# A four-portion decoder trunk: the odd portions' convolution counted out per pair of experts, and one norm divided later

## The chip, the cores and the metric

One core of a Trainium2 chip runs the whole program. The metric is the device time of one execution in microseconds (us), the median of three runs.

## The reference, cut to what matters

Two layers run over 256 prompt rows and 32 sample rows of 1024 channels. Each layer is a mixing sublayer (three parallel branches and their gates) and an expert sublayer, which looks up 16 of 16384 one-neuron experts for each of 8 heads.

```python
glu = val_b * jax.nn.sigmoid(gate_b)
ext = jnp.concatenate([conv_past, glu], axis=1)
c = _causal_depthwise(ext, w['b_conv_w'], w['b_conv_b'])      # 31 taps
y_b = jax.nn.silu(_layernorm(c, w['b_ln_g'], w['b_ln_b']))
merged = (jax.nn.sigmoid(gl_a) * (y_a @ w['w_o_a'])
          + jax.nn.sigmoid(gl_b) * (y_b @ w['w_o_b'])
          + jax.nn.sigmoid(gl_m) * (y_m @ w['w_o_m']))
x = x + merged @ w['w_out']
...
hid = jax.nn.gelu(jnp.einsum('bd,bhkd->bhk', xb, u_tab[eid]), approximate=False)
return jnp.einsum('bhk,bhkd->bd', g * hid, v_tab[eid])        # g: softmax of the 16 best scores
```

The change touches when the 31-tap depthwise convolution is done and when its LayerNorm is divided. What is computed stays the same.

## The kernel before

The rows are cut into four portions `m` = 0 to 3: portion 0 is layer 0 of the first 128 prompt rows, portion 1 is layer 0 of the other 128 and of the 32 sample rows, and 2 and 3 are the same for layer 1. Each portion has a mixing part (function `mixing(m)`, one for each engine) and an expert part. The expert part is a row of pairs: even portions have 8 steps of 8 pairs (64 pairs), odd portions 10 steps (80 pairs). For a pair GpSimd (POOL) issues two gathers of 1 MB each (line L611) into one of five slots, VectorE (DVE) forms two dot products (`dots`, L1672), ScalarE (ACT) applies gelu and builds two diagonals (`diags`, L1036), and TensorE (PE) multiplies them with the gathered rows (`values`, L2453), which frees the slot.

While the pairs of portion `m` run, the mixing part of portion `m + 1` is done beside them. There is no scheduler on the chip: a table `PLACE[m]` gives every piece of the mixing part a place on a scale worked out from estimated costs (`glu0` .. `glu7`, attention `S`, `T`, `O`, gates `mg0` .. `mg23`, the spatial pieces `ua` and `sg`, `csum` and `csq` for the convolution's norm, `out`, `wq`, `sc`), and `reach(m, u)` says how far along it an engine may go by pair `u`. A generator per engine yields places, and the engine runs it up to `reach` after each pair. PE goes one pair further than DVE and ACT: it does mixing work after the value products of pair `u`, which DVE and ACT meet after the dot products of pair `u + 1`. Every engine runs its own list in order, so an instruction that waits holds all behind it on its engine.

On DVE the order within a pair is: dot products; then one of the selection's parts by the pair's number `k` in its step (`k` = 0 `pick_pairs`, 1 `pick_experts`, 3 `gates`, 5 `scale_fold`, 6 and 7 `pick_half`; at `k` = 2 and 4 there is none, and the mixing part goes there); for `k` = 2 of every other step `add_group` (L1695); then the mixing part up to `reach`. The convolution of 31 taps over 8 blocks of 128 channels is cut into 62 steps of four instructions each (`convolve`, L1141 for the first tap, L1143 for the others). In the kernel before, the mixing code itself calls `conv(taps)` with small numbers, in front of its attention, gate and spatial pieces, and a last `conv(2 * CONV_W)` in front of `centre` takes what is left. The sample rows' convolution runs beside `glu`: POOL multiplies (L638, four products per block of channels) and DVE sums (`sample_taps`, L1151).

The norm behind the convolution is `centre` (`csum`, L1448), ACT's squares, and `norm_c` (`csq`): DVE scales PE's sum of squares (L1454), ACT takes the root, DVE takes its reciprocal (L1456) and multiplies (L1458), and ACT's `swish` follows. Pairs are counted below from the start of the expert part beside which the mixing runs, from 0 to 63 beside portions 0 and 2.

Of the kernel before, what the change touches and what calls it, by code (L numbers as in the profile page):

```python
# [19 lines left out]
CONV_W = 31  # L20
# [10 lines left out]
PORTIONS = 2 * DEPTH  # L31
# [5 lines left out]
STEPS = (8, 10)  # L37
FIRST = [sum(STEPS[i % 2] for i in range(m)) for m in range(PORTIONS + 1)]
NSTEP = FIRST[PORTIONS]
PAIRS = 8  # L40
# [26 lines left out]
CACHED = (0, 3)  # L67
# [27 lines left out]
for _k, _c in WKIND:  # L95
# [14 lines left out]
    conv=(1, 1), pe_csum=(1, 1), cd=(1, 1), csq=(1, 1), pe_csq=(1, 1), cvar=(1, 1), rt_c=(1, 1), cn=(1, 1), yb=(8, 8),  # L110
# [16 lines left out]
def at(name, m, k):  # L127
    return sum(per(name, i) for i in range(m)) + k
# [61 lines left out]
PLACE = []  # L190
# [27 lines left out]
def reach(m, u):  # L218

    last = PAIRS * STEPS[(m - 1) % 2] - TAIL  # L220
    place = PLACE[m]
    if u >= last:

        return place.get(f"sc{u - last + 1}", 1e9)
    if m == 1:

        return place["glu0"] + (place["sc1"] - place["glu0"]) * (u + 1) / (last + 1)
    return place["sc1"] * (u - LEAD) / (last - LEAD)

# [11 lines left out]
def build(nc, x_in, consts_in, mem_in, cache_in, state_in, w_in, small_in, vecs_in, fing_in, ws_in, wss_in,  # L241
          keys_in, uv_in, y_out, memk_out, memv_out, convp_out, convs_out, vn_out):
    with ExitStack() as ctx:
# [857 lines left out]
        def _(dve):  # L1101
# [29 lines left out]
            def mixing(m):  # L1131
# [21 lines left out]
                done = [0]  # L1153

                def conv(n):

                    for _ in range(n):
                        if done[0] < 2 * CONV_W:
                            convolve(4 * (done[0] // CONV_W), (done[0] % CONV_W,))
                            done[0] += 1  # L1160

# [24 lines left out]
                for c in range(KB):  # L1186
# [17 lines left out]
                    if m == 0 and c == 2:  # L1204
                        dve.wait_ge(S["memsq"], 1)
                        V.tensor_reduce(rb_mem, kT.rearrange("p c t -> p t c"), AX.X, ALU.add).then_inc(S["memred"], 1)
                    if p == 0 and c == (4 if m == 0 else 2):
                        dve.wait_ge(S["pe_memsq"], at("pe_memsq", m, 1))
                        V.tensor_scalar(rb_mem, s_bank[0][:, 0:M], 1.0 / D, EPS, ALU.mult, ALU.add).then_inc(S["memvar"], 1)
# [35 lines left out]
                def beside(name, taps):  # L1245
                    yield place[name]
                    conv(taps)
# [44 lines left out]
                else:  # L1292
# [35 lines left out]
                    if m == 1:  # L1328
                        conv(2)
# [22 lines left out]
                def gated(first, last, taps):  # L1352
                    for c in range(first, last):

                        yield place[f"mg{c + 1}"] + 2 if c % 8 == 0 else place[f"mg{c}"]
                        conv(taps)
# [63 lines left out]
                def spatial():  # L1420
                    for i in range(3):
                        yield from beside(f"ua{i}", 1 if m == 3 else 2)
                    for i in range(4):
# [3 lines left out]
                        conv((2, 1, 2, 0)[m])  # L1427
# [23 lines left out]
                def norm_c():  # L1451
                    yield place["csq"]
                    dve.wait_ge(S["pe_csq"], at("pe_csq", m, 1))
                    V.tensor_scalar(rb[:, 0:nt], t_bank[:, 0:nt], 1.0 / D, EPS, ALU.mult, ALU.add).then_inc(S["cvar"], 1)  # L1454
                    dve.wait_ge(S["rt_c"], at("rt_c", m, 1))
                    V.reciprocal(rb[:, 0:nt], rb[:, 0:nt])  # L1456
                    dve.drain()
                    V.tensor_tensor(yB[:, :, 0:nt], yB[:, :, 0:nt], rb[:, 0:nt].unsqueeze(1).to_broadcast([P, KB, nt]), ALU.mult).then_inc(S["cn"], 1)  # L1458
# [19 lines left out]
                else:  # L1478
                    taps = 1 if m in CACHED else 2
                    yield from gated(0, 3, taps)  # L1480
                    yield from norm_v_gain()
                    yield from gated(3, 5, taps)
                    yield from norm_v_bias()
                    yield from gated(5, 8, taps)
                    yield from spatial()
                    yield from gated(8, 12, 3 if m in CACHED else 4)
                    conv(2 * CONV_W)
                    yield from centre()
                    yield from gated(12, 14, 0)
                    yield from norm_c()  # L1490
                    yield from gated(14, 24, 0)
# [245 lines left out]

            V.memset(one, 1.0).then_inc(one_set, 1)
# [9 lines left out]
            for m in range(PORTIONS):  # L1748
                mix = first if m == 0 else stepper(mixing(m + 1)) if m + 1 < PORTIONS else None
                for u in range(PAIRS * STEPS[m % 2]):  # L1750
# [22 lines left out]
                    if k == 2 and s % 2 == 0 and s:  # L1773
                        add_group(s // 2 - 1)
                    if mix:
                        mix(reach(m + 1, u - 1))
# [796 lines left out]
```

## Time and profile before

| | us |
|---|---|
| median of 3 runs (lowest, highest) | 2237.01 (2234.17, 2238.07) |
| the profiled execution | 2238.65 |
| its span, first to last instruction | 2236.9 |
| PE busy | 1631.0 (73%) |
| DVE busy | 1567.8 (70%) |
| POOL busy | 721.5 (32%) |
| ACT busy | 656.0 (29%) |

The DMA engines moved 895.56 MB at 400 GB/s on average. The page cuts the span into 40 equal slices of 56 us. A group or row of the trace names the line, the engine, the operation, what it writes and reads, and in brackets how long the engine stood idle before it and what it then got. Matmul ends are modelled, so a busy PE is not a PE at its peak.

### The profile page before, as it was taken

To read this page: it belongs to the slowest core of one execution; us is meant where nothing else is said; L and a number is where in the kernel's file an instruction comes from. 1 tells how busy PE (TensorE), PEld (TensorE's weight loads), DVE (VectorE), ACT (ScalarE), POOL (GpSimd) and SP (SyncE) were. 2 spreads that over 40 slices of the span, in tenths; PEclk is the share of its full clock that TensorE was granted. 3 is DMA by queue.
4 is the path that set the end of the run, shared out by engine and by line. 5 is a ranking of instruction groups with operands and counts; after the bars stand their busy time and mean duration, and the time that the engine had idled before them with its cause. 6 is when DMAs were issued, how large, how long until landed. Compare 5 with 4: busy or idle time off the path is not lost.

```text
span 2236.9 us, 31355 instructions
## 1 busy us (share of the span) xinstructions
PE 1631.0 (73%) x10944; PEld 1069.0 (48%) x10944; DVE 1567.8 (70%) x4170; ACT 656.0 (29%) x1647; POOL 721.5 (32%) x660
## 2 busy tenths in 40 slices
PE   9999987788797477878788647766999853334334
PEld 9866675566675055554433415543887610000002
DVE  4464269988766667877775577787876686776775
ACT  3121232421414242432132323342223332322222
POOL 0000056332232433342222234531323254454443
PEclk9999998899898588999899757876999865555556
DMA  9699899999899999999999999999999999999997
GB/s 338 250 385 402 335 406 420 384 418 400 327 410 419 422 420 421 422 412 422 421 390 421 421 421 414 409 393 396 420 417 421 409 400 421 422 421 421 422 421 317
DMA packets 127773, 895.56 MB, mean 400 GB/s; under 512 B 16096, under 2 KB 16928, under 8 KB 20480
## 3 DMA queue, kind: packets, MB, share of 16 engines
q0 software_dynamic: 83232, 604.02, 65.6%
q1 hardware_dynamic: 44384, 289.54, 32.1%
q8 instruction: 88, 1.44, 0.3%
q14 instruction: 69, 0.57, 0.1%
HBM read 885.39 MB, written 8.11 MB: 399 GB/s over the span
## 4 chain that ended last, share of the span: by engine, by line
PE 33%; DMA 28%; DVE 24%; issue 4%; ACT 4%; DVEq 3%; POOL 3%; SPq 0%; POOLq 0%; ACTq 0%
DMA uv<-uv_in,idx_u 22%; PE bank L1797 14%; DVE uv L1672 11%; PE bank L2109 5%; PE bank L2453 4%; DMA ring<-w_in 4%; DVE yB L1143 3%; PE bank L1803 3%; POOL uv L611 2%; DMA ring<-cache_in 2%; POOL merged L638 1%; ACT L675 1%; DVEq L1138 1%; ACT diag L1036 1%; DVE x L1695 1%
## 5 line engine op out<-in xcount | busy, mean ns | idle before, releaser
L611 POOL DMA_INDIRECT uv<-uv_in,idx_u x574 | 652.1, 1136 | 1294.5 <-PE bank L2453 634.1
L1672 DVE CUSTOM_DVE_ANT_0 uv<-uv,xrep 128x1024 f32<-128x1024 f32 x576 | 687.4, 1231 | 217.0 <-DMA uv<-uv_in,idx_u 209.6
L2453 PE MATMUL bank<-uv,diag 128*32 128x512 f32 x2176 | 393.0, 803 | 476.2 <-ACT diag L1036 470.3
L1797 PEld LDWEIGHTS bank<-xnT,ring 128*128 128x128 f32 x3168 | 434.5, 202 | 77.4 <-issue 68.3
L1797 PE MATMUL bank<-xnT,ring 128*128 128x160 f32 (+1 forms) x3168 | 456.2, 304 | 1.1 <-DMA ring<-w_in 1.0
L675 ACT ACTIVATE pick<-pick 128x2 f32<-128x2 f32 (+1 forms) x315 | 66.9, 213 | 1053.3 <-DVE pick L1672 1052.5
L2453 PEld LDWEIGHTS bank<-uv,diag 128*32 128x32 f32 x2176 | 49.4, 122 | 663.3 <-ACT diag L1036 598.0
L1143 DVE SCALAR_TENSOR_TENSOR yB<-ext_p,small,yB 128x128 f32<-128x128 f32 x960 | 275.2, 348 | 19.5
L675 ACT ACT_TABLE_LOAD x137 | 175.8, 1283 | 2.4
L1036 ACT ACTIVATE diag<-gated_fold,pick 128x32 f32<-128x32 f32 x574 | 153.1, 314 | 9.8 <-ACT pick L675 0.5
L2109 PE MATMUL bank<-ring,xnT 128*128 128x512 f32 x192 | 88.3, 615 | 0.0
L1797 PE MATMUL bank<-yMA,ring 128*128 128x160 f32 x512 | 76.8, 306 | 5.5 <-ACT yMA L675 5.5
L1797 PEld LDWEIGHTS bank<-yMA,ring 128*128 128x128 f32 x512 | 73.6, 196 | 5.7 <-ACT yMA L675 5.7
L675 ACT ACTIVATE phase<-bank 128x512 f32<-128x512 f32 (+2 forms) x44 | 23.3, 529 | 176.4 <-PE bank L1797 73.4
L1020 ACT ACTIVATE xrep<-xnf 32x1024 f32<-32x1024 f32 x64 | 67.4, 1053 | 1.4
L1803 PE MATMUL bank<-ring,ext_s 128*128 128x256 f32 x256 | 60.9, 399 | 0.0
L2446 PE MATMUL bank<-uv,diag 128*32 128x256 f32 x256 | 28.2, 586 | 43.0 <-ACT diag L1036 43.0
L2109 PEld LDWEIGHTS bank<-ring,xnT 128*128 128x128 f32 x192 | 36.8, 196 | 47.1 <-issue 46.2
L2109 PE MATMUL bank<-ring,yMA 128*128 128x512 f32 x128 | 57.0, 597 | 0.5 <-DMA ring<-w_in 0.3
L675 ACT ACTIVATE sg<-bank 128x160 f32<-128x160 f32 (+1 forms) x80 | 23.4, 293 | 115.1 <-PE bank L1797 114.9
L1797 PE MATMUL bank<-ext_s,ring 128*128 128x256 f32 x256 | 57.1, 381 | 0.0
L1803 PEld LDWEIGHTS bank<-ring,ext_s 128*128 128x128 f32 x256 | 51.1, 202 | 12.1 <-issue 4.6
(323 smaller groups left out, 1848.0 us busy)
## 6 DMA issues: line engine op xcount, KB each, us to landing
ring<-w_in SPq DMA_DIRECT2D x211, 1024.0 KB
uv<-cache_in SPq DMA_DIRECT2D x16, 1024.0 KB, 9.6
ring<-cache_in SPq DMA_DIRECT2D x16, 1024.0 KB
uv<-uv_in,idx_u POOLq DMA_INDIRECT x578, 13.9
uv<-w_in SPq DMA_DIRECT2D x4, 1024.0 KB, 10.3
ring<-w_in SPq DMA_DIRECT2D x6, 512.0 KB, 4.7
ext_s<-state_in SPq DMA_DIRECT2D x2, 1088.0 KB, 14.0
convs_out<-ext_s SPq DMA_DIRECT2D x2, 1088.0 KB, 24.7
```

What stands on the lines that cost most here:

```text
L611: nc.gpsimd.indirect_dma_start(out=uvbuf[2 * b + i], out_offset=None, in_=uv_in, in_offset=bass.IndirectOffsetOnAxis(ap=ids[:, c:c + 1], a ...
L638: ins = nc.gpsimd.tensor_tensor(taps_s[:, :, t], ext_s[:, c, :, t:t + CONV_W], wconv[:, c].unsqueeze(1).to_broadcast([P, NSEQ, CONV_W]), A ...
L675: ins = nc.scalar.activation(out, in_, func, bias=bias, scale=scale, **({} if accum is None else {"accum_out": accum}))
L1020: ins = nc.scalar.activation(xrep[gg % 2][32 * i:32 * (i + 1), :], xnf[1 if t == 2 else 0][r0:r0 + 32], ACT.Copy)
L1036: ins = nc.scalar.activation(diag[:, t % 4, i], gated_fold[:, c], ACT.Copy, scale=gel[:, 16 * (s % 2) + c:16 * (s % 2) + c + 1])
L1143: ins = V.scalar_tensor_tensor(out=yB[:, c, 0:P], in0=ext_p[:, c, w:w + P], scalar=wconv[:, c, w:w + 1], in1=yB[:, c, 0:P], op0=ALU.mult, ...
L1672: ins = V.tensor_tensor_reduce(out=u, in0=u, in1=xrep[gg % 2][:, :], scale=1.0, scalar=0.0, op0=ALU.mult, op1=ALU.add, accum_out=hid[:, c: ...
L1797: ins = MM(out, w[:, k, P * b:P * (b + 1)], rhs(k), start=k == 0, stop=k == KB - 1)
L1803: ins = MM(out, lhs(k), w[k], start=k == 0, stop=k == KB - 1)
L2109: ins = MM(out[:, :], rows[:, 4 * (i % 2) + k, 0:P], w[:, k, :], start=i % 2 == 0 and k == 0, stop=i % 2 == 1 and k == 3)
L2446: ins = MM(vbank[gg % 2][32 * q:32 * (q + 1), 0:256], diag[:, t % 4, i], uvbuf[2 * b + i][:, c:c + 256], start=first and i == 0, stop=last ...
L2453: ins = MM(vbank[gg % 2][c:c + 32, :], diag[:, t % 4, i], uvbuf[2 * b + i][:, D + 512 * n:D + 512 * (n + 1)], start=first, stop=last)
```

## The change

In odd portions (1 and 3) the convolution no longer hangs on the mixing code. `TAPS[m][u]` says how many of the 62 steps are to be done by the end of pair `u`; it shares them by the weights `HEAVY` over the pairs from the one that reaches `glu4` to two before the one that reaches `csum`. DVE calls `conv_upto` once a pair, behind the selection's part and `add_group` and ahead of the last mixing call. A step waits until `glued` says that its four blocks of `glu` are there. All other `conv` calls of odd portions fall away, but for the last one, which finds nothing left. Even portions keep theirs. The second part: in odd portions `norm_c` yields at place `mg14` between its scaling and the wait for ACT's root.

```diff
+HEAVY = (1, 1, 3, 3, 4, 3, 1, 1)
+
+def taps_by(m):
+    us = range(PAIRS * STEPS[(m - 1) % 2])
+    first = next(u for u in us if reach(m, u - 1) >= PLACE[m]["glu4"])
+    last = next(u for u in us if reach(m, u - 1) >= PLACE[m]["csum"]) - 2
+    total, so_far, out = sum(HEAVY[u % PAIRS] for u in range(first, last + 1)), 0, []
+    for u in us:
+        so_far += HEAVY[u % PAIRS] if first <= u <= last else 0
+        out.append(-(-2 * CONV_W * so_far // total))
+    return out
+
+TAPS = {m: taps_by(m) for m in range(1, PORTIONS, 2)}
...
-                done = [0]
+                done, glued = [0], [0]
...
+                def conv_upto(n):
+                    while done[0] < n and glued[0] >= 4 * (done[0] // CONV_W + 1):
+                        conv(1)
+                if p:
+                    beside_pair[0] = conv_upto
...
+                    glued[0] = c + 1
...
                 def beside(name, taps):
                     yield place[name]
-                    conv(taps)
+                    if p == 0:
+                        conv(taps)
...
-                def gated(first, last, taps):
+                def gated(first, last):
                     for c in range(first, last):
                         yield place[f"mg{c + 1}"] + 2 if c % 8 == 0 else place[f"mg{c}"]
-                        conv(taps)
                         dve.wait_ge(S["pe_proj"], at("pe_proj", m, c + 1))
...
-                        conv((2, 1, 2, 0)[m])
+                        conv((2, 0, 2, 0)[m])
...
                     V.tensor_scalar(rb[:, 0:nt], t_bank[:, 0:nt], 1.0 / D, EPS, ALU.mult, ALU.add).then_inc(S["cvar"], 1)
+                    if p:
+                        yield place["mg14"]
                     dve.wait_ge(S["rt_c"], at("rt_c", m, 1))
                     V.reciprocal(rb[:, 0:nt], rb[:, 0:nt])
...
+                    if m % 2 == 0:
+                        beside_pair[0](TAPS[m + 1][u])
                     if mix:
                         mix(reach(m + 1, u - 1))
```

The steps done in each pair, read from the two orders of DVE (four instructions each):

| portion, pairs | before | after |
|---|---|---|
| 1, 0 to 7 | 0 0 0 0 0 0 0 0 | 0 0 0 0 5 3 1 1 |
| 1, 8 to 15 | 0 4 2 2 2 1 2 3 | 1 1 3 3 4 3 1 1 |
| 1, 16 to 23 | 0 2 0 4 2 2 2 2 | 1 1 3 3 4 3 1 1 |
| 1, 24 to 31 | 2 2 2 4 1 2 2 9 | 1 1 3 3 4 3 1 1 |
| 1, 32 and 33 | 4 4 | 1 0 |
| 3, 8 to 15 | 0 0 0 0 3 1 2 2 | 0 2 3 3 4 3 1 1 |
| 3, 16 to 23 | 3 3 1 3 5 2 3 6 | 1 1 3 3 4 3 1 1 |
| 3, 24 to 31 | 4 0 3 1 1 1 1 2 | 1 1 3 3 4 3 1 1 |
| 3, 32 to 37 | 1 1 1 0 6 6 | 1 1 3 3 3 0 |

The lists of PE, ACT, POOL and SP keep their order. First place: DVE in portion 1, pair 5, the sum of a sample block. `yB` is the convolution's result, `merged` holds POOL's products, `gated_fold` the experts' weights. Before:

```order
L1672 ISA uv,pick<-uv,xrep 128x1024
L1672 ISA pick 128x1
L1684 TENSOR_TENSOR gated_fold<-consts,pick 128x256
L1151 TENSOR_REDUCE yB<-merged 128x32
L1199 TENSOR_TENSOR ext_p<-bank,sg 128x128
```

And now (line numbers of the changed kernel), from the end of pair 4:

```order
L1161 SCALAR_TENSOR_TENSOR yB<-ext_p,small,yB 128x128 x16
L1698 ISA uv,pick<-uv,xrep 128x1024
L1698 ISA pick 128x1
L1710 TENSOR_TENSOR gated_fold<-consts,pick 128x256
L1161 SCALAR_TENSOR_TENSOR yB<-ext_p,small,yB 128x128 x12
L1169 TENSOR_REDUCE yB<-merged 128x32
```

Four plus three steps moved ahead of this sum, and with the first tap's four instructions pair 4 holds five steps.

Second place: DVE in portion 1, pair 31, the last spatial product (`yMA`) and the gates 8 and 9 (`sg`, `merged`). Before:

```order
L1143 SCALAR_TENSOR_TENSOR yB<-ext_p,small,yB 128x128 x4
L1439 TENSOR_TENSOR yMA<-yMA,bank 128x320
L1143 SCALAR_TENSOR_TENSOR yB<-ext_p,small,yB 128x128 x16
L1364 SCALAR_TENSOR_TENSOR sg<-sg,bank 128x160
L1366 TENSOR_TENSOR merged<-merged,sg 128x160
L1143 SCALAR_TENSOR_TENSOR yB<-ext_p,small,yB 128x128 x16
L1364 SCALAR_TENSOR_TENSOR sg<-sg,bank 128x160
```

And now:

```order
L1161 SCALAR_TENSOR_TENSOR yB<-ext_p,small,yB 128x128 x4
L1464 TENSOR_TENSOR yMA<-yMA,bank 128x320
L1389 SCALAR_TENSOR_TENSOR sg<-sg,bank 128x160
L1391 TENSOR_TENSOR merged<-merged,sg 128x160
L1389 SCALAR_TENSOR_TENSOR sg<-sg,bank 128x160
```

The two runs of four steps each that stood between the product and the gates are gone.

Third place: DVE in portion 1, pairs 36 and 37, the norm (`rb` is the root's row). Before:

```order
L1454 TENSOR_SCALAR rb<-bank 128x160
L1456 RECIPROCAL rb<-rb 128x160
L1458 TENSOR_TENSOR yB<-yB,rb 128x1280
L1672 ISA uv,pick<-uv,xrep 128x1024
L1672 ISA pick 128x1
```

And now:

```order
L1479 TENSOR_SCALAR rb<-bank 128x160
L1698 ISA uv,pick<-uv,xrep 128x1024
L1698 ISA pick 128x1
L1710 TENSOR_TENSOR gated_fold<-consts,pick 128x256
L1483 RECIPROCAL rb<-rb 128x160
L1485 TENSOR_TENSOR yB<-yB,rb 128x1280
```

The dot products of pair 37 and its fold moved ahead of the wait for the root. In portion 3 both places are reached by the same pair, so nothing stands between the two parts there.

## Rows read from the trace of the kernel before

**Rows 1.** The page, part 2: DMA share and rate in 40 slices.

```profile
DMA  9699899999899999999999999999999999999997
GB/s 338 250 385 402 335 406 420 384 418 400 327 410 419 422 420 421 422 412 422 421 390 421 421 421 414 409 393 396 420 417 421 409 400 421 422 421 421 422 421 317
```

**Rows 2.** Windows: stretch, length, busy us by engine, PE clock, DMA share, GB/s.

```profile
295.00:360.00 65.00, 54.00 (x384) 44.17 (x382) 50.82 (x126) 19.40 (x53) 45.82 (x49) 0.97 1.01 421
360.00:430.00 70.00, 52.87 (x540) 37.96 (x540) 65.50 (x187) 26.98 (x75) 27.60 (x23) 0.85 1.02 419
430.00:570.00 140.00, 112.58 (x728) 92.07 (x728) 123.02 (x357) 31.92 (x85) 36.07 (x34) 0.88 0.95 381
570.00:646.00 76.00, 68.75 (x473) 56.40 (x470) 49.43 (x117) 30.05 (x68) 22.44 (x22) 0.96 0.95 375
```

**Rows 3.** Timeline of DVE: start, us, instructions; two convolution steps.

```profile
463.20 2.35 DVE L1143 SCALAR_TENSOR_TENSOR yB<-ext_p,small,yB 128x128 f32<-128x128 f32 x8
```

**Rows 4.** Timeline of DVE, portion 1: two sums of the sample convolution.

```profile
327.89 1.19 DVE L1151 TENSOR_REDUCE yB<-merged 128x32 f32<-128x992 f32 x1 [1.85 <-POOL merged L638]
...
334.20 1.19 DVE L1151 TENSOR_REDUCE yB<-merged 128x32 f32<-128x992 f32 x1 [1.22 <-POOL merged L638]
```

**Rows 5.** Timelines of DVE and POOL: a dot product and four products, beside and apart.

```profile
342.89 1.68 DVE L1672 CUSTOM_DVE_ANT_0 uv<-uv,xrep 128x1024 f32<-128x1024 f32 x1
...
360.99 1.22 DVE L1672 CUSTOM_DVE_ANT_0 uv<-uv,xrep 128x1024 f32<-128x1024 f32 x1
...
319.14 2.56 POOL L638 TENSOR_TENSOR merged<-ext_s,small 128x248 f32<-128x248 f32 x4
...
330.25 3.92 POOL L638 TENSOR_TENSOR merged<-ext_s,small 128x248 f32<-128x248 f32 x4
```

**Rows 6.** Timelines of DVE and PE, portion 1, pairs 28 to 34.

```profile
511.51 0.49 DVE L1439 TENSOR_TENSOR yMA<-yMA,bank 128x320 f32<-128x320 f32 x1 [2.34 <-PE bank L2166]
...
531.78 0.49 DVE L1439 TENSOR_TENSOR yMA<-yMA,bank 128x320 f32<-128x320 f32 x1 [1.77 <-PE bank L2166]
532.36 4.78 DVE L1143 SCALAR_TENSOR_TENSOR yB<-ext_p,small,yB 128x128 f32<-128x128 f32 x16
...
569.43 1.49 DVE L1448 SCALAR_TENSOR_TENSOR yB<-bank,yB 128x1280 f32<-128x1280 f32 x1 [1.25 <-PE bank L2178]
...
533.95 4.51 PE L1797 MATMUL bank<-yMA,ring 128*128 128x160 f32 x32
...
565.32 4.07 PE L2178 MATMUL bank<-yB,consts 128*128 128x160 f32 x16 [5.76 <-DVE yB L1143]
```

**Rows 7.** Timelines of DVE and ACT, portion 1, pairs 36 to 38.

```profile
586.27 1.15 DVE L1456 RECIPROCAL rb<-rb 128x160 f32<-128x160 f32 x1 [3.27 <-ACT rb L675]
587.85 1.49 DVE L1458 TENSOR_TENSOR yB<-yB,rb 128x1280 f32<-128x1280 f32 x1 [0.43 <-issue]
...
591.67 0.20 ACT L675 ACTIVATE pick<-pick 128x2 f32<-128x2 f32 x1 [4.13 <-DVE pick L1672]
...
601.72 0.30 ACT L675 ACTIVATE sg<-bank 128x160 f32<-128x160 f32 x1
```

**Rows 8.** Windows of portion 3, columns as in rows 2.

```profile
1424.00:1460.00 36.00, 24.83 (x199) 20.06 (x199) 31.34 (x96) 10.56 (x24) 11.35 (x11) 0.86 1.00 394
1460.00:1474.00 14.00, 14.00 (x200) 10.42 (x202) 10.29 (x31) 11.17 (x28) 6.52 (x6) 1.00 0.93 334
...
1636.00:1662.00 26.00, 22.53 (x153) 19.57 (x153) 23.92 (x71) 5.53 (x15) 6.64 (x6) 0.91 1.01 421
```

**Rows 9.** Timeline of DVE, portion 3, pairs 11 and 16.

```profile
1418.92 1.19 DVE L1151 TENSOR_REDUCE yB<-merged 128x32 f32<-128x992 f32 x1 [1.29 <-POOL merged L638]
...
1462.66 0.42 DVE L1234 TENSOR_REDUCE stat<-bank 128x1 f32<-128x256 f32 x1 [2.06 <-PE bank L1929]
...
1464.09 0.16 DVE L1241 RECIPROCAL stat<-stat 128x1 f32<-128x1 f32 x1 [0.77 <-ACT merged L675]
```

**Rows 10.** The chain that ended last, portion 3: start, us, what.

```profile
1489.05 20.18 DMA ring<-cache_in
```

More of the change, by code:

```diff
@@ L1327, in mixing @@
                     yield place["va3"]
-                    if m == 1:
-                        conv(2)
                 for t in range(1 + p):
@@ L1478, in mixing @@
                 else:
-                    taps = 1 if m in CACHED else 2
-                    yield from gated(0, 3, taps)
+                    yield from gated(0, 3)
                     yield from norm_v_gain()
-                    yield from gated(3, 5, taps)
+                    yield from gated(3, 5)
                     yield from norm_v_bias()
-                    yield from gated(5, 8, taps)
+                    yield from gated(5, 8)
                     yield from spatial()
-                    yield from gated(8, 12, 3 if m in CACHED else 4)
+                    yield from gated(8, 12)
                     conv(2 * CONV_W)
                     yield from centre()
-                    yield from gated(12, 14, 0)
+                    yield from gated(12, 14)
                     yield from norm_c()
-                    yield from gated(14, 24, 0)
+                    yield from gated(14, 24)
                 for i in range(4):
@@ L1736, in layer @@
                 return next(i for i in range(PORTIONS) if s < FIRST[i + 1]) // 2
+            beside_pair = [None]
             V.memset(one, 1.0).then_inc(one_set, 1)
```

## The prediction

> **What bounds the kernel now.** I began with the page's rate row: from the fifth slice the DMA engines move about 421 GB/s wherever nothing keeps them from it, and the row has only a few dips [rows 1]. What lies outside the dips can't be won by another order on VectorE (DVE), since the bytes stay the same. So a change of order is worth the DMA time that it gives back, and costs the DMA time that it leaves empty. The dips beside which the change works are two in portion 1's mixing and a smaller one in portion 3's.
>
> Windows over portion 1 show them [rows 2]. From 295 to 430 us the DMA is full (421 and 419 GB/s). From 430 to 570 us it moves 381 GB/s, from 570 to 646 us 375 GB/s. Against 421 GB/s that is 140 x 40/421 = 13.3 us and 76 x 46/421 = 8.3 us, together 21.6 us, the most that portion 1 can give. DVE is busy 123.0 of the 140 us and 65.5 of the 70 us before: it is the bound there. In the last window it is busy only 49.4 of 76 us and TensorE (PE) 68.8: there PE and its round trips bind. In portion 3 the DMA loses 14 x 87/421 = 2.9 us between 1460 and 1474 us, and nothing between 1636 and 1662 us [rows 8], where the kernel before has its last burst of 6 and 6 steps.
>
> A step of the convolution (four instructions) takes 2.35/2 = 1.18 us [rows 3]. Their number doesn't change, 62 a portion, 73 us each. DVE being the bound up to the end of portion 1's convolution, evening them out shortens nothing by itself: what counts is which of DVE's waits are filled, and which are uncovered.
>
> **The change part by part, portion 1.** The table of steps says that the new order runs ahead of the old by 10 steps at the end of pair 7, by 8 to 16 up to pair 30, and is level again after pair 33. So DVE comes 9 to 19 us later to every piece of mixing in between, and makes it up in pairs 31 to 33.
>
> (a) Waits for POOL's products. The wait of 1.22 us in pair 5 [rows 4] is filled by the 5 steps of pair 4 and 3 of pair 5: -1.2 us. The wait of 1.85 us in pair 4 stays: at k = 4 the mixing call comes first and the steps come behind it, though they would have covered it.
>
> (b) The steps of pair 4 now run beside POOL's products. The trace of before has no convolution step there, but it has dot products, which also read two tensors in SBUF: 1.68 us beside them and 1.22 us apart, and POOL's four products take 3.92 us instead of 2.56 us [rows 5]. So the two hold each other up. Bounds for the steps of pair 4: nothing, and one product ahead of a step for each of the four, 4 x 0.64 = 2.6 us. The nearest row is the dot product's, 0.46 us for one; three such, +1.4 us.
> The Trainium skill (SBUF — State Buffer, Who interferes with whom) says that a DVE instruction with two SBUF inputs and a GpSimd instruction that reads SBUF take turns on a shared port, one blocked until the other ends. By that rule the steps, whose inputs both lie in SBUF, are held as the dot products are, and it speaks against this change; without it term (b) would be 0 and the sum 1.4 us lower. The trace agrees for the dot products [rows 5]; no row of before shows a step beside a product.
>
> (c) Cover in front of the spatial pieces and gates, pairs 28 to 34. In pair 28 DVE waits 2.34 us for the first spatial product [rows 6]. In front of it stood 2 + 4 + 1 = 7 steps since the dot products of pair 26, now 3 + 3 = 6, and the 4 of pair 28 come behind: the wait grows by a step to 3.5 us. In pair 31 PE can only start the 32 matmuls for gates 8 and 9 (4.51 us) when DVE has made the last product, and 4 + 4 steps of 4.78 us hid them [rows 6]. Now both gates follow at once: 4.51 us and the tanh behind it, less what DVE does for gate 8 meanwhile, 4.6 us of wait. The waits of 0.24 and 1.77 us (the latter in rows 6) go, since in pairs 30 and 31 DVE comes later against PE. Waits before 2.34 + 0.24 + 1.77 = 4.35, after 3.5 + 4.6 = 8.1: +3.75 us. Against it, the steps are done in pair 32, so that PE sums them without the 5.76 us that it stood for DVE, and DVE's own wait of 1.25 us in `centre` goes [rows 6]. (c) is +2.5 us. Bounds: 0 (PE has other work in hand) and +5.
>
> (d) The norm. DVE stands 3.27 + 0.43 us for the root [rows 7]. Now it has the dot products of pair 37 (2.4 us) and a fold (0.4 us) to do first, so the wait is filled. ACT gets the dot products 6 us sooner: 2.64 us of division and 3.70 us of wait no longer lie ahead of them, and it stood 4.13 us for them [rows 7]. The division itself is done at the same time as before, but ACT's gelu and diagonals are over by then, so that swish starts about 4 us sooner, and with it the tanh of gate 15, at 601.72 us before, which is what DVE and then PE wait for. -4 us; bounds -6.3 (both items whole) and 0 (ACT's chain of root, table loads and swish sets the end anyway).
>
> (e) Pairs 9 to 25. The attention's maxima and gates 0 to 7 had two steps in front of each and nearly no wait. At k = 2 and 4 they now have none. PE needs a value product and a piece of mixing behind DVE's last dot products, about 7 us, and DVE spends about 7 us a pair: it just fits. Bounds 0 and +3, I take +1.
>
> Portion 1: -1.2 + 1.4 + 2.5 - 4 + 1 = -0.3 us.
>
> **Portion 3.** The new order starts at pair 9 instead of 12. Up to the maximum in pair 16 it has 18 steps behind it and the old one 9: 9 x 1.18 = 10.6 us later. Filled: the wait for POOL of 1.29 us in pair 11, and the waits of 2.06 and 0.77 us in pair 16 [rows 9]. Added: steps beside products in pairs 10 and 12, 0 to 2 x 2.6 us, I take +2. In pairs 16 and 17 the new order has 1 further step and the old one 5: -4.7 us. The dot products of pair 18 come 10.6 - 1.3 - 2.8 + 2 - 4.7 = +3.8 us later. From there PE takes in the cached keys, and a DMA chain of 20.18 us follows [rows 10]. Loads that are under way may cover part of it; the bounds are -2.9 (the dip between 1460 and 1474 us is evened out) and +7; I take +2 us. The relief at pairs 36 and 37 is worth 0, because the DMA is full there. The norm in portion 3 isn't split, both places being reached by one pair: 0.
>
> **Sum.** -0.3 + 2 = +1.7 us on the profiled execution's 2238.65 us (span 2236.9 and 1.75 around it) gives 2240.3. The median of the runs lies 1.6 us below the profiled one, so 2238.7 us. A difference within 0.2% (4.5 us) is about what a measurement of this kernel can't tell from none; this forecast lies in it.
>
> **Rivals.**
> Faster: evening out works for PE more than I count. PE stood 5.76 us for the last step, and its sum then took 4.07 us at a clock that had fallen, the DMA lost 21.6 us around there [rows 2, 6]. If half of that comes back: -10.8 us, 2226 to 2232. For it speaks that the dips follow the bursts of steps; against it that DVE is the bound (123.0 of 140 us) and none of its work goes.
> Slower: the late start of the mixing. The steps ahead of time push PE's pieces and so its weight loads back by 9 to 19 us, while the DMA was full in just that stretch (421 and 419 GB/s [rows 2]); time that it stands empty there is paid. In both portions, with the upper bounds of (b) and of the steps beside products (+1.2 and +3.2), of (e) (+2) and portion 3's lateness uncovered (+1.8 more): +8, 2247. It decides from the point where DVE's lateness exceeds what four weight loads and five slots hold in stock. For it: the rows of rivalry with POOL [rows 5]; against it: the order is level again by pair 33 in portion 1, and the waits in pairs 16 to 21 of portion 3 take in lateness.
> No effect of the norm's split: ACT's root, table loads and swish set gate 15 whatever DVE does. Then (d) is 0 and the time 2242.7, within or just over the bound.
>
> **How the numbers follow.** The forecast with its own terms, 0.43; faster, 0.25; slower by the late start, 0.20; the norm's split without effect, 0.12, which falls half within 0.2% and half over it. The ends of the terms reach from -9 to +15 us; each end needs all of them at once, so the range for 8 in 10 is 2229 to 2250. Faster by over 0.2% 0.26, within 0.44, slower 0.30.
>
> **What would show it.** In the profile after: no wait for POOL in pair 5, dot products or steps longer than 1.22 and 0.3 us beside L638's successor; in pair 31 a wait of about 4 us at gates 8 and 9; PE's column sum of the convolution without a wait for DVE; the root's wait gone and the tanh of gate 15 some 4 us nearer to the division; DMA below 421 GB/s already before 430 us, and less below it from 430 to 570. The forecast is wrong if the DMA's loss over portion 1 falls by more than 5 us, or if it moves below 410 GB/s in the stretch before 430 us without getting it back later.

## The result, and the profile after

| | before | after |
|---|---|---|
| median of 5 runs each (lowest, highest), us | 2235.87 (2234.17, 2238.07) | 2254.56 (2252.20, 2256.53) |
| the profiled execution, and its span | 2238.65, 2236.9 | 2253.72, 2251.9 |

The ratio is 1.0082, 95% interval 1.0067 to 1.0096: the change costs 18.3 us. The forecast was 2238.7 within 2229 to 2250, no change the likeliest. It was wrong.

The same windows as before the change [rows 2, 8], and one more of each kernel (stretch, length, busy us by engine, PE clock, DMA share, GB/s). After:

```profile
295.00:360.00 65.00, 50.48 (x325) 40.25 (x323) 54.92 (x149) 17.84 (x48) 37.19 (x39) 0.87 0.96 393
360.00:430.00 70.00, 51.74 (x469) 37.77 (x468) 62.81 (x178) 26.01 (x71) 29.11 (x32) 0.85 1.01 390
430.00:570.00 140.00, 119.28 (x823) 97.00 (x821) 116.37 (x332) 32.06 (x89) 38.66 (x35) 0.89 0.93 371
570.00:646.00 76.00, 68.04 (x459) 56.69 (x456) 51.26 (x121) 31.34 (x69) 25.04 (x22) 0.93 1.01 418
...
1424.00:1460.00 36.00, 22.58 (x114) 17.13 (x115) 29.36 (x78) 8.63 (x20) 14.69 (x18) 0.72 0.88 324
...
1390.50:1722.70 332.20, 262.50 (x2068) 203.01 (x2067) 249.41 (x683) 100.94 (x247) 107.14 (x104) 0.89 0.98 399
```

Before, pairs 8 to 43 of portion 3:

```profile
1384.50:1707.30 322.80, 261.76 (x2068) 202.43 (x2067) 248.40 (x683) 101.45 (x247) 109.21 (x104) 0.88 1.00 409
```

Over those 36 pairs of portion 3 the engines do the same work (DVE 248.4 and 249.4 us, PE 261.8 and 262.5) and nearly the same bytes move, at 399 instead of 409 GB/s and in 9.4 us more. In portion 1 the DMA, full up to 430 us before, now moves 393 and 390 GB/s there, 371 instead of 381 up to 570 us, and then 418 instead of 375: part of what it lost comes back in the last window. No work was added. DVE waits more.

**A ledger by pair.** Where the waits grew can be read off the starts of each pair's dot products. They come later than before by the steps that were done ahead of time, 1.18 us each [rows 3], and that is no loss. So I subtract it: loss = start after - start before - 1.18 x steps ahead. All kernels below, which the next section describes, are set against the one profile of before. Changes along a row are what to read, and only the larger ones: kernels differ by 1 or 2 us at pair 4 of portion 1, where they do the same, and the split alone and the steps into waits, which have one order in portion 3, differ there by 3.5 us over pair 26 alone (-3.9 and -0.4).

| loss in us at the start of pair | p1: 4 | 20 | 30 | 32 | 38 | p3: 8 | 26 | 27 | 36 | 38 | 44 |
|---|---|---|---|---|---|---|---|---|---|---|---|
| after | -0.6 | -0.5 | -1.4 | +6.8 | +5.2 | +6.0 | +0.8 | +11.4 | +9.2 | +17.2 | +15.4 |
| split alone | -1.1 | -1.1 | -1.3 | -3.4 | -6.6 | -5.4 | -5.3 | -9.2 | -9.2 | -9.1 | -10.0 |
| k = 2, 4 first | -1.5 | -1.5 | -8.0 | -4.0 | -7.0 | -2.0 | -8.1 | +0.1 | -4.4 | +4.4 | +2.5 |
| before's numbers | -1.0 | -1.2 | +0.5 | +5.6 | +2.6 | +1.7 | +4.2 | +5.1 | +7.1 | +11.9 | +11.3 |
| steps into waits | +1.6 | +1.6 | -3.6 | -5.8 | -10.3 | -9.0 | -8.7 | -9.1 | -9.1 | -9.0 | -10.1 |

The first row has three jumps, and each is a group of waits. Pairs 30 and 31 of portion 1, +8.2 us, DVE after (the last spatial products, gates 8 and 9):

```profile
541.90 0.49 DVE L1464 TENSOR_TENSOR yMA<-yMA,bank 128x320 f32<-128x320 f32 x1 [1.29 <-PE bank L2195]
...
550.49 0.49 DVE L1464 TENSOR_TENSOR yMA<-yMA,bank 128x320 f32<-128x320 f32 x1 [2.90 <-PE bank L2195]
555.45 0.32 DVE L1389 SCALAR_TENSOR_TENSOR sg<-sg,bank 128x160 f32<-128x160 f32 x1 [4.47 <-ACT sg L693]
...
557.62 0.32 DVE L1389 SCALAR_TENSOR_TENSOR sg<-sg,bank 128x160 f32<-128x160 f32 x1 [1.45 <-ACT sg L693]
```

That is 10.1 us of waits. Before there was the one of 1.77 [rows 6]: 8.3 more. The two kernels with the same steps in portion 1 jump by 7.0 (steps alone) and 5.5 us (portion 1 counted) here, so the size is known to a few us. Pair 26 of portion 3, +10.6 us, gates 0 to 2, after:

```profile
1569.43 0.32 DVE L1387 SCALAR_TENSOR_TENSOR merged<-sg,bank 128x160 f32<-128x160 f32 x1 [12.47 <-ACT sg L693]
1571.60 0.32 DVE L1387 SCALAR_TENSOR_TENSOR merged<-sg,bank 128x160 f32<-128x160 f32 x1 [1.85 <-ACT sg L693]
1577.14 0.32 DVE L1387 SCALAR_TENSOR_TENSOR merged<-sg,bank 128x160 f32<-128x160 f32 x1 [5.21 <-ACT sg L693]
1577.56 3.57 DVE L1161 SCALAR_TENSOR_TENSOR yB<-ext_p,small,yB 128x128 f32<-128x128 f32 x12
```

and before:

```profile
1564.04 0.32 DVE L1362 SCALAR_TENSOR_TENSOR merged<-sg,bank 128x160 f32<-128x160 f32 x1 [4.31 <-ACT sg L675]
1566.21 0.32 DVE L1362 SCALAR_TENSOR_TENSOR merged<-sg,bank 128x160 f32<-128x160 f32 x1 [0.62 <-ACT sg L675]
1571.75 0.32 DVE L1362 SCALAR_TENSOR_TENSOR merged<-sg,bank 128x160 f32<-128x160 f32 x1 [3.98 <-ACT sg L675]
```

19.5 us of waits against 8.9, the ledger's 10.6. Both kernels do three steps in this pair: before one in front of each gate, after all three behind the last (the row of 3.57 us).

But a jump is not yet a loss. From pair 8 to pair 26 the same row falls by 5.2 us: DVE ran ahead there and then stood at this gate. The gates wait for PE, and PE for the cached keys' loads; the last of its waits for them, before and after:

```profile
1550.16 1.93 PE L2000 MATMUL bank<-ring,ext_s 128*32 128x256 f32 x16 [3.10 <-DMA ring<-cache_in]
```

```profile
1555.43 1.93 PE L2029 MATMUL bank<-ring,ext_s 128*32 128x256 f32 x16 [3.07 <-DMA ring<-cache_in]
```

Counted from the start of pair 8, these rows lie at 165.67 and 164.95 us and gate 2 at 187.3 and 186.7. In all 18 profiles of this case gate 2 comes 183.5 to 188.3 us behind pair 8, with 36 to 47 steps done by then. So what counts is how many of the 62 steps are done by gate 2: 41 before, 36 now. Two of the five are missing from the numbers per pair (38 and 36 by the end of pair 25), three by their place in pair 26. Five steps are 5.9 us, and the ledger moves by 5.4 from pair 8 to pair 27.

Pairs 36 and 37, +8.0 us, gates 8 to 10, after:

```profile
1663.38 0.32 DVE L1389 SCALAR_TENSOR_TENSOR sg<-sg,bank 128x160 f32<-128x160 f32 x1 [4.45 <-ACT sg L693]
...
1665.56 0.32 DVE L1389 SCALAR_TENSOR_TENSOR sg<-sg,bank 128x160 f32<-128x160 f32 x1 [1.45 <-ACT sg L693]
...
1674.55 0.32 DVE L1389 SCALAR_TENSOR_TENSOR sg<-sg,bank 128x160 f32<-128x160 f32 x1 [1.97 <-ACT sg L693]
```

With the fourth, of 0.18, they make 8.05 us, where the kernel before had three steps in front of each gate and no wait at all. Of the 8.0, 2.1 come back in pair 38, whose gate cost the kernel before 3.68 us of wait and now 1.60.

### The profile page after: what moved, and what is told of

It is laid out like the page before. It is cut to its first block, busy times and chain, and to the rows that moved or that the text cites. A ratio compares the mean times of both kernels' runs of the same rounds, so it can differ in the third digit from the quotient of the medians.

```text
span 2251.9 us, 31355 instructions
## 1 busy us (share of the span) xinstructions
PE 1636.5 (73%) x10944; PEld 1073.9 (48%) x10944; DVE 1568.6 (70%) x4170; ACT 655.1 (29%) x1647; POOL 724.2 (32%) x660
## 4 chain that ended last, share of the span: by engine, by line
DMA 30%; PE 28%; DVE 27%; ACT 5%; issue 4%; DVEq 4%; POOL 2%; SPq 0%; POOLq 0%; ACTq 0%
DMA uv<-uv_in,idx_u 24%; PE bank L1826 13%; DVE uv L1698 12%; PE bank L2138 5%; DVE yB L1161 4%; PE bank L2482 4%; DMA ring<-w_in 3%; PE bank L1832 2%; DMA ring<-cache_in 2%; ACT L693 1%; POOL uv L629 1%; DVEq L1156 1%; ACT diag L1054 1%; DVE x L1721 1%; POOL merged L656 1%
## 5 line engine op out<-in xcount | busy, mean ns | idle before, releaser
L1826 PEld LDWEIGHTS bank<-xnT,ring 128*128 128x128 f32 x3168 | 441.1, 204 | 85.3 <-issue 74.2
L1826 PE MATMUL bank<-xnT,ring 128*128 128x160 f32 (+1 forms) x3168 | 463.4, 307 | 8.4 <-DMA ring<-w_in 3.1
L656 POOL TENSOR_TENSOR merged<-ext_s,small 128x248 f32<-128x248 f32 x64 | 54.1, 876 | 27.4 <-DVE yB L1169 27.2
```

The lines of the kernel that those rows point to most:

```text
L656: ins = nc.gpsimd.tensor_tensor(taps_s[:, :, t], ext_s[:, c, :, t:t + CONV_W], wconv[:, c].unsqueeze(1).to_broadcast([P, NSEQ, CONV_W]), A ...
L1826: ins = MM(out, w[:, k, P * b:P * (b + 1)], rhs(k), start=k == 0, stop=k == KB - 1)
```

## The experiments

The first column is the median of 4 to 11 executions. The second is the difference from the kernel before measured beside it, worked out from the ratio times 2236, with the 95% interval; for eleven steps that kernel stood at 2237.9 us, elsewhere at 2235.0 to 2236.3, so compare by the second column. Theory P: the losses belong to the parts and add up. Theory L: a step is free in front of a piece that waits for PE and costs 1.18 us anywhere else. Its rivals stand in the expectations. The edits are shown cut to what matters.

| run | us | against before |
|---|---|---|
| after | 2254.6 | +18.3 (15.0, 21.5) |
| split alone | 2233.3 | -2.5 (-4.5, -0.4) |
| steps alone | 2257.5 | +20.6 (17.0, 23.9) |
| portion 1 counted, split | 2243.8 | +7.4 (4.7, 10.1) |
| portion 3 counted, split | 2244.9 | +9.6 (6.5, 12.5) |
| before's numbers | 2249.7 | +13.4 (10.3, 16.5) |
| k = 2 and 4 first | 2239.8 | +3.6 (1.6, 5.6) |
| k = 4 alone first | 2248.8 | +13.9 (10.7, 16.8) |
| p3, late burst | 2247.8 | +11.4 (8.5, 14.5) |
| p3, late burst in threes | 2244.6 | +6.0 (3.4, 8.7) |
| p3, ten steps ahead of gate 0 | 2238.1 | +1.8 (-0.2, 3.8) |
| p1 counted, k = 2 and 4 first | 2236.6 | +0.2 (-1.8, 2.2) |
| the same from pair 9 | 2235.0 | -0.2 (-2.2, 1.8) |
| p3 mended | 2233.8 | -2.0 (-4.0, 0.0) |
| both mended | 2237.6 | +1.6 (-0.4, 3.6) |
| five steps into waits | 2227.6 | -7.6 (-10.3, -4.9) |
| eleven steps into waits | 2229.3 | -7.6 (-10.3, -4.9) |

**The parts.** Split alone (the mixing code's own `conv` calls back in both portions), steps alone, and each portion counted by itself:

```diff
 # split alone; for one portion counted, the lines hold for the other portion only
-                    if p == 0:
-                        conv(taps)
+                    conv(taps)
...
-                    beside_pair[0] = conv_upto
 # steps alone
-                    if p:
-                        yield place["mg14"]
```

> The steps as in the kernel before, only the norm of the odd portions in two parts. Before 2235.9 us, after 2254.6. Theory P (each part costs what it costs where the two traces part: portion 1's steps +9.3 us, the split -4.1, portion 3's steps +10, and they add up): 2232 us, the root's wait of 3.27 us gone and the tanh of gate 15 about 4 us earlier against the division. Rival R (the split brings nothing, ACT's chain sets the end): 2236.

> The steps counted per pair in both portions as in the changed kernel, the norm in one part as before. Theory P: 2235.9 + 9.3 + 10 = 2255 to 2259 us, and the wait for the root is back in portion 1. Rival R (the split brings nothing): 2254.6, and the same start of the pairs behind the norm as in the changed kernel.

> Portion 1 counted per pair with the split, portion 3 with the steps of the kernel before. Theory P (portion 3's 10 us are made by its own steps): 2235.9 + 9.3 - 4.1 = 2241 us. Rival Q (portion 3 inherits its loss from portion 1's lateness, by buffers and loads that come late): about 2250 us, with the +10 us still arising between pairs 26 and 36 of portion 3.

> Portion 3 counted per pair, portion 1 with the steps of the kernel before and the split. Theory P: 2235.9 - 4.1 + 10 = 2242 us, and the wait of about 12 us at the gate of pair 26 of portion 3 is there. Rival Q: 2232 to 2236 us, no such wait.

Steps of portion 1: 7.4 + 2.5 = 9.9 us. Steps of portion 3: 9.6 + 2.5 = 12.1. With the split's -2.5 that makes 19.5, and 18.3 was measured. P holds: portion 3's loss is its own, Q falls (12.1 us with portion 1 as before). The split is worth 2.5 us by itself, by an interval that just excludes 0, so R falls too. In the changed kernel it is 20.6 - 18.3 = 2.3 us, which the two intervals can't tell from none. The division's row with the steps alone, and with the split alone (start, us, wait in brackets):

```profile
594.73 1.15 DVE L1486 RECIPROCAL rb<-rb 128x160 f32<-128x160 f32 x1 [3.27 <-ACT rb L694]
```

```profile
583.78 1.15 DVE L1488 RECIPROCAL rb<-rb 128x160 f32<-128x160 f32 x1 [0.65 <-ACT rb L694]
```

**Number or place.** The changed kernel with before's numbers per pair, with the steps first at both positions, and at k = 4 only:

```diff
 # before's numbers
+TAPS[1], TAPS[3] = the running sums of the table's rows "before"
 # k = 2 and 4 first (k = 4 alone: "and k == 4" added)
                     elif mix:
+                        if m % 2 == 0:
+                            beside_pair[0](TAPS[m + 1][u])
                         mix(reach(m + 1, u - 1))
```

> The changed kernel with one thing altered: each pair does as many steps as it does in the kernel before (0 4 2 2 ... 9 4 4), but all in one place, where the changed kernel has them, and not in front of the mixing's pieces; split as in the changed kernel. The split alone is 2233.3 us, the changed kernel 2254.6. Theory N (the numbers per pair are what costs): within 3 us of 2233.3. Rival L (the place within the pair costs: steps no longer stand in front of the pieces that wait for PE, behind them at k = 2 and 4): 2245 to 2255, with waits of DVE for PE at gates and spatial pieces as in the changed kernel.

> The changed kernel, but at k = 2 and 4 too the steps come ahead of the mixing call and not behind it. Numbers per pair as in the changed kernel. Rival L: most of the loss goes, 2240 us or less. Theory N: the loss stays, 2250 to 2255 us, since the waits filled at k = 2 and 4 are worth a step or two each.

> The changed kernel with the steps ahead of the mixing call at k = 4 only; at k = 2 they stay behind it. Both ahead took 2239.8 us, none 2254.6. By the waits in the changed kernel's trace, k = 4 holds portion 1's (3.78 and 1.92 us), k = 2 the long one at gate 0 in pair 26 of portion 3 (12.47 us). Theory L, by these waits: 2244 to 2250, portion 1 cured and portion 3 not. If k = 2 alone matters: above 2252.

Before's numbers at the new place: still +13.4, 15.9 us over the split alone. So it isn't evenness that costs, and N falls. Nor is it lateness: with the changed kernel's numbers but the steps first, 14.7 of the 18.3 us are gone, though the mixing still comes up to 15.3 us late. In pair 20 of portion 1 the changed kernel has

```profile
462.67 0.32 DVE L1387 SCALAR_TENSOR_TENSOR merged<-sg,bank 128x160 f32<-128x160 f32 x1 [3.78 <-ACT sg L693]
...
466.69 4.78 DVE L1161 SCALAR_TENSOR_TENSOR yB<-ext_p,small,yB 128x128 f32<-128x128 f32 x16
```

a wait and then the four steps that would have filled it, and with the steps first:

```profile
458.30 4.78 DVE L1162 SCALAR_TENSOR_TENSOR yB<-ext_p,small,yB 128x128 f32<-128x128 f32 x16 [0.45 <-issue]
462.99 0.32 DVE L1392 SCALAR_TENSOR_TENSOR merged<-sg,bank 128x160 f32<-128x160 f32 x1
```

k = 4 alone heals portion 1 (its loss at pair 38 is -8.4 us) and leaves portion 3 (11.2 us from pair 8 to 44; 9.4 in the changed kernel), as L said. Of the -8.4 there are -2.8 left at pair 60, where the DMA runs full. With the steps first at k = 2 as well, gate 0 of pair 26 in portion 3 still waits 10.04 us and the ledger jumps by 8.2: 39 steps done by gate 2, two short of 41, and 2.1 us lost from pair 8 to 27.

**Portion 3.** Portion 1 as before with the split. The last 12 steps in pairs 36 and 37 at one place each, the same three in front of each gate 8 to 11, and ten steps brought forward to pair 25:

```diff
 # late burst: from pair 27 on, until pair 35, 11 steps and not 20
+TAPS[3][27:37] = 40, 41, 42, 43, 45, 46, 47, 48, 50, 56
 # in threes: TAPS[3] stops at 50, and in gated
+                        elif m == 3 and 8 <= c < 12:
+                            conv(3)
 # ahead of gate 0: TAPS[3] at least 46 from pair 25 on
```

> Portion 1 as before with the split; portion 3 counted per pair as in the changed kernel up to pair 26, and from there as few as before with the rest (6 and 6) in pairs 36 and 37. The same without this edit (portion 3 counted throughout) took 2244.9 us, portion 3 as before 2233.3. Theory B (the burst of before lies behind PE's gates 8 to 11, where DVE would have waited anyway, and the 14 steps moved ahead of it lie where DVE is the bound): 2233 to 2237 us. Rival W (the lost time is the wait of 12.47 us at pair 26, made by what came earlier): still 2242 to 2246, with the wait there.

> As the run with the late burst (2247.8 us: portion 1 as before with the split, portion 3 counted, its last 12 steps in pairs 36 and 37), but those 12 steps stand three in front of each of the gates 8 to 11, as in the kernel before, and not six at one place of a pair. Theory L (what counts is what a step stands in front of: the burst was free in the kernel before because it lay behind PE's gates): 7 us come back, 2240 to 2242. Rival M (the burst costs by its number, wherever in the pair it stands): 2246 to 2249.

> Portion 1 as before with the split; portion 3 as in the changed kernel, but 10 steps of pairs 26 to 28 are done in pair 25, ahead of the gate for which DVE stood 12.47 us in the changed kernel. Without this edit 2244.9 us. Theory W (time lost in that wait): 2233 to 2237, the wait down to 1 us or less. Rival B (the wait is slack that is made up later or is made by DMA-bound weights of PE; what counts is the burst at the end): 2241 to 2246, because DVE reaches pair 36 no sooner.

The late burst did not bring back anything: theory B, mine from comparing the two traces, falls. Its ledger jumps by 7.0 us in pair 36, because the six steps of pair 36 (k = 4) stand behind its gates (start, us, wait in brackets):

```profile
1647.98 0.32 DVE L1395 SCALAR_TENSOR_TENSOR sg<-sg,bank 128x160 f32<-128x160 f32 x1 [5.36 <-ACT sg L695]
1650.15 0.32 DVE L1395 SCALAR_TENSOR_TENSOR sg<-sg,bank 128x160 f32<-128x160 f32 x1 [1.45 <-ACT sg L695]
...
1650.97 7.21 DVE L1163 SCALAR_TENSOR_TENSOR yB<-ext_p,small,yB 128x128 f32<-128x128 f32 x24
```

In threes the one wait left in these pairs is 1.75 us and the jump 1.8, and the time falls by 5.4 us, under the 7 expected. Ten steps ahead of gate 0 take 7.8 us off (2238.1 us, 1 us above the range expected). Gate 0 then has no wait, and gates 1 and 2 read

```profile
1564.37 0.32 DVE L1393 SCALAR_TENSOR_TENSOR merged<-sg,bank 128x160 f32<-128x160 f32 x1 [0.70 <-ACT sg L695]
1569.90 0.32 DVE L1393 SCALAR_TENSOR_TENSOR merged<-sg,bank 128x160 f32<-128x160 f32 x1 [5.21 <-ACT sg L695]
```

By gate 2 this kernel has done 46 steps, five more than before, and the ledger moves by -5.2 us from pair 8 to 27 where the changed kernel's moves by +5.4; the other five with 36 by then move by +6.1 to +7.0, the one with before's numbers, 38, by +3.4, and the five with portion 3 as before, 41, by -0.1 to -3.8. No run moved the loads of the cached keys themselves, so that they set the gates' time is read from the rows and from this agreement.

**Mending both.**

```diff
 # portion 3 mended: k = 2 and 4 first; 46 steps by pair 25, 50 by 35, then
+                        elif m == 3 and 8 <= c < 12:
+                            conv(3)
 # both mended: as well, TAPS[1] stops at 57 and
+                        elif m == 1 and c in (8, 9):
+                            conv(4 if c == 8 else 1)
 # from pair 9: TAPS[1] shared by HEAVY over pairs 9 to 32
```

> Portion 1 counted per pair and split as in the changed kernel, but the steps ahead of the mixing call at k = 2 and 4 too; portion 3 as before. With the steps behind the call this took 2243.8 us, with portion 1 as before and the split 2233.3. Theory L: 2233 to 2236 us, DVE's waits of 3.78 us (gate 7) and 1.92 us (spatial product of pair 28) filled, the mixing still up to 19 us late in between. Rival E (the early start itself, beside POOL's products and PE's weight loads, costs what it seems to): 2239 or more.

> Portion 1 as before with the split. Portion 3: steps ahead of the mixing call, 10 of them brought forward into pair 25 in front of gate 0, few in pairs 26 to 35, the last 12 three in front of each of the gates 8 to 11. Against portion 3 as before (2233.3 us): by theory L all waits of DVE for PE are covered and fewer steps stand where DVE is the bound (pairs 26 to 35): 2227 to 2233 us. If the early steps of pairs 9 to 15, beside POOL's products, cost by themselves: 2236 to 2239.

> Portion 3 as in the run before this one; portion 1 counted, steps ahead of the mixing call, and 5 of the steps kept back for the gates 8 and 9 of pair 31, for which DVE stood 4.47 and 1.45 us. Theory L: as the mended portion 3 with portion 1 as before, or up to 4 us less; 2225 to 2232. Rival: the waits at gates 8 and 9 are paid back later anyway, then the same as without keeping steps back.

> As the run with portion 1 counted and its steps ahead of the mixing call (2236.6 us), but the counting starts at pair 9 and not 4, so that no step stands beside POOL's products or in the stretch before 430 us where the DMA fell from 420 to 397 and 390 GB/s; portion 3 as before. Portion 1 as before with the split is 2233.3. Theory S (the early start is what is left of portion 1's loss, 3.3 us): 2231 to 2234 us, and 415 GB/s or more from 295 to 360. Rival G (what is left is the bare gates 8 and 9 in pair 31, 5.9 us of wait): 2236 to 2238.

(The gate of pair 20, called gate 7 in the first of these, is gate 2.) Portion 1 with the steps first comes to within 2.7 us of the split alone, and portion 3 mended to within 0.5: cured or nearly, and no better than before's own order. Mending both missed L's forecast (2225 to 2232): the steps kept back for gates 8 and 9 left waits of 3.36 and 3.25 us at the last two spatial products in place of theirs, and the time is that of the two parts added. Where portion 1's last 2.7 us arise is not settled. Its pairs run level with the split alone up to 44, then the dot products of pair 46 wait for their gather:

```profile
646.16 1.23 DVE L1704 CUSTOM_DVE_ANT_0 uv<-uv,xrep 128x1024 f32<-128x1024 f32 x1 [6.00 <-DMA uv<-uv_in,idx_u]
```

By pair 49 all but 0.9 us of this is made up again, and in pairs 59 to 63 the kernel stands 3.5 to 3.9 us behind the split alone, though from 646 to 760 us the DMA moves 419 GB/s or more in both. This kernel, like the changed one, moved only 392 and 397 GB/s up to 430 us. The start at pair 9 has no such wait, but gained less before it (-4.3 us at pair 38, not -7.1), and its time can't be told from the other's: S and G stay open.

**Steps into waits.** The kernel before with the split, and five of portion 1's last steps moved, then six of portion 3's as well:

```diff
-                        conv(taps)
+                        conv(taps + (3 if m == 1 and c == 2 else 0))
...
-                        conv((2, 1, 2, 0)[m])
+                        conv((2, 3 if i == 0 else 1, 2, 0)[m])
 # eleven steps: "or m == 3 and c in (0, 2)" added
```

> The kernel before with the split, and 5 steps of the last ones of portion 1 moved: 3 in front of gate 2 in pair 20 (a wait of 2.77 and then 1.12 us), 2 in front of the first spatial product in pair 28 (2.33 us). Against 2233.3 us: theory L (a step is free in front of a wait and dear where DVE is the bound): up to 6 us less, 2227 to 2231. Rival: PE's late pieces shift with DVE and the waits open again behind, 2232 to 2235.

> As the run that moved five steps of portion 1 into waits (2227.6 us), and portion 3 likewise: 3 steps in front of gate 0 and 3 in front of gate 2 in pair 26, for which DVE stood 3.97 and 3.98 us, taken from the last burst of pair 37 in front of gates 10 and 11. Theory L alone: up to 6 us less, 2222 to 2226. Rival D (around the burst the DMA moved 421 GB/s, so time won there is not time won at the end, and only the dips from 1540 to 1572 us can give): 2225 to 2228. Rival C (gates 10 and 11, now bare, cost what was won): 2227 to 2231.

Five steps moved: 5.1 us less than the split alone, 7.6 us less than the kernel before (ratio 0.9966, 0.9954 to 0.9978). It is the fastest order found. Pair 20 has five steps and no wait at gate 2, and 0.47 us in place of 1.12 behind it:

```profile
445.70 6.00 DVE L1162 SCALAR_TENSOR_TENSOR yB<-ext_p,small,yB 128x128 f32<-128x128 f32 x20
451.61 0.31 DVE L1392 SCALAR_TENSOR_TENSOR merged<-sg,bank 128x160 f32<-128x160 f32 x1
```

The six of portion 3 add nothing. The ledger's start of pair 37 comes 10.8 us earlier than with five. Gates 10 and 11, now bare, wait 1.97 and 1.28 us, so that 7.6 are left at pair 38; this is rival C, and it is a part. The rest is gone by pair 48 (0.8 left), in waits for gathers:

```profile
1712.82 1.23 DVE L1704 CUSTOM_DVE_ANT_0 uv<-uv,xrep 128x1024 f32<-128x1024 f32 x1 [2.92 <-DMA uv<-uv_in,idx_u]
1722.87 1.22 DVE L1704 CUSTOM_DVE_ANT_0 uv<-uv,xrep 128x1024 f32<-128x1024 f32 x1 [5.35 <-DMA uv<-uv_in,idx_u]
```

Rival D accounts for the larger part: beside a DMA at 421 GB/s, time won is lent. The run's time lies in C's range and, set against the kernel measured beside it, could be either's; the trace tells them apart.

Of the nine runs for which L named a time, five came slower than its range (in threes, p1 with the steps first, p3 mended, both mended, eleven steps), by 0.6 to 5.6 us, and none faster. It tells where a step is dear, and promises too much for moving it.

## Why the prediction was wrong

The step that failed is the sentence on portion 3, "The relief at pairs 36 and 37 is worth 0, because the DMA is full there", and with it the sum of +2 us for portion 3. The steps that went from there were the cover of gates 8 to 11. Bare, these cost 8.0 us at pair 38. With three steps in front of each gate again (the burst in threes) 5.4 us of the time came back. The full DMA there [rows 8] was, as I now read it, the sign that the cover worked, not that it was not needed. And the gates of pair 26 stand in no term at all: their waits grew by 10.6 us, and five steps fewer are done by gate 2, 5.4 us of loss since pair 8. I compared the numbers per pair, which are 3 and 3 there, and neither the sum up to that gate nor what each step stands in front of. Portion 3's steps cost 12.1 us, over the upper bound of +7. The lateness that I did count there came as said (+4.5 us at pair 18, forecast +3.8) and cost nothing by gate 2.

Portion 1 came to +7.4 us where I had -0.3; there (c) is the term that was too small. The ends of my terms add up to -10.4 and +16.4 us, not to -9 and +15 as I wrote. Even +16.4 is less than the 18.3 measured: a term was missing, not only sizes wrong.

By its own terms:

- (a) right: no wait for POOL is left in pair 5. (b) right in kind: the five steps of pair 4 beside POOL's products took 7.85 us. Alone they take 1.12 + 4.78 = 5.90, so +1.95, where I said +1.4 and at most 2.6. The rows, after and (last) before:

```profile
328.91 2.24 DVE L1159 TENSOR_SCALAR yB<-ext_p,small 128x128 f32<-128x128 f32 x4
331.23 5.53 DVE L1161 SCALAR_TENSOR_TENSOR yB<-ext_p,small,yB 128x128 f32<-128x128 f32 x16
```

```profile
369.00 1.12 DVE L1141 TENSOR_SCALAR yB<-ext_p,small 128x128 f32<-128x128 f32 x4
```

 The Trainium skill (SBUF — State Buffer, Who interferes with whom) has it that a DVE instruction with two SBUF inputs and a GpSimd instruction that reads SBUF contend for a shared port. The trace agrees for the sixteen with two such inputs, which overlap POOL's products in part (5.53 us, 4.78 alone). The four of the first tap read one tensor and lost more, 2.24 us against 1.12; that rule does not cover them. The ledger stands at -0.5 in pair 20, where it began, so that all this cost nothing by then.
- (c) wrong in size. The gates' wait of 4.6 us came as 4.47 and 1.45. The first spatial wait shrank to 1.92 where I had 3.5. But "the waits of 0.24 and 1.77 us go, since DVE comes later against PE" failed: they are 1.29 and 2.90. PE was later still. It stood for ACT's diagonals of pair 29, whose dot products come behind the four steps of pair 28, which follow the mixing call, and then ran at a lower clock (below). Waits of 12.0 us in all against 4.35: +7.7, over the bound of +5 before the 1.25 us of `centre` are taken off, and over it after.

```profile
531.37 1.93 PE L2482 MATMUL bank<-uv,diag 128*32 128x512 f32 x8 [3.01 <-ACT diag L1054]
```

- (c), last part, right: PE sums the convolution without a wait (570.08, 2.44 us, where it took 4.07 after 5.76 of idling [rows 6]).
- (d) right where it was placed. The root's wait is 0.65 us, and the tanh of gate 15 follows the division by 606.89 - 595.56 = 11.3 us, before by 15.45 [rows 7]: 4.1 us nearer. The ledger falls by the same 4.1 us from pair 36 to 38, and by 0 in the kernel with the steps alone. Of these 2.5 and 2.3 us reach the end.
- (e) Pairs 9 to 25: I took +1. The ledger goes from -0.9 at pair 9 to -1.2 at pair 26. But gate 2's wait in pair 20, which four steps could have filled, stayed; with them in front the loss falls by 3.8 us.

Of the rivals, the slower one was nearest in size (2247) and wrong in its mechanism: lateness as such costs little, as the run with the steps first shows (3.6 us in all, with the mixing up to 15.3 us late). The faster one saw a true thing, that this dip can give 5 us or more, but by filling waits and not by evening out. Of the two signs named for a wrong forecast one did not come: the DMA's loss from 430 to 646 us fell by 4.4 us, less than 5. The other came in part: 393 and 390 GB/s before 430 us cost 9.1 us of the DMA's time and the stretch up to 570 us another 3.3, of which the last window gave 7.8 back.

## What to carry to other kernels

In this kernel filler work had a cost by its place and not by the piece: nearly free where it is done ahead of a wait for another engine, up to the length of that wait, and close to its full length elsewhere. Where the end of the wait does not hang on the waiting engine, as at gate 2 of pair 26, what counts is how much is done by then, not in which pair. So before work is evened out, list for each wait of the engine how much is done ahead of it, and compare two orders by that list and not by how much is done per unit. Where the DMA is full behind a place, count time won there as lent until the next gather has been looked at.

## What the runs showed of the hardware

Behind a short stand of PE its clock was low. After the 3.01 us ahead of pair 29's value products the granted clock was 0.53 and 0.61 for 20 us, and in the second half of them the DMA moved 283 GB/s. After:

```profile
520.00:530.00 10.00, 8.36 (x60) 6.60 (x56) 7.76 (x22) 0.73 (x3) 3.75 (x4) 1.00 1.01 419
530.00:540.00 10.00, 8.63 (x33) 6.11 (x34) 9.08 (x31) 1.79 (x7) 2.04 (x2) 0.53 1.01 419
540.00:550.00 10.00, 10.00 (x46) 7.67 (x45) 6.00 (x19) 0.74 (x3) 0.88 (x1) 0.61 0.68 283
```

With the steps first, the same pairs:

```profile
521.00:531.00 10.00, 9.01 (x56) 7.20 (x56) 9.60 (x28) 1.74 (x7) 3.88 (x4) 0.89 1.01 419
531.00:541.00 10.00, 10.00 (x56) 8.60 (x56) 8.34 (x29) 0.79 (x4) 1.89 (x2) 0.77 1.01 420
```

0.53 and 0.61 are means near the lower of the two levels, 1.2 GHz of 2.4. The kernels with the steps alone and with portion 1 counted have the same stand (3.01 and 3.00 us); counted from the start of pair 28, their clock from 10 to 30 us was 0.70 and 0.62, 0.81 and 0.68, where the changed kernel has 0.60 and 0.54 and the one with the steps first, without such a stand, 0.74 and 0.92. So the clock dips without the stand too, and over these 20 us it was lower with it. That the clock fell because of this wait is how I read the order of events; no run held PE back by itself.
